# Expert weights laid out per partition, gate and up in one transfer, and the token table summed on TensorE

## The chip, the cores and the metric

The kernel runs on one core of one Trainium2 chip. The metric is the device time of one execution in microseconds (us), the median of the runs shown; lower is better.

## What is computed

A block of 512 tokens (D = 1024, float32) passes two models in a row: a mixer, a cross attention and a mixture of experts, then twice a token mixer with four branches and a mixture of experts. Only the three expert layers bear on the change. Each has 32 experts in four groups; a token goes to the best group and to the best two experts in it. An expert's hidden width is 512 in the first layer and 256 in the other two.

```python
    order = jnp.argsort(e_flat)
    e_sorted, t_sorted, w_sorted = e_flat[order], t_flat[order], w_flat[order]
...
    def expert_block(args):
        xb, e = args
        return (jax.nn.silu(xb @ w_gate[e]) * (xb @ w_up[e])) @ w_down[e]
...
    contrib = (w_sorted[:, None] * y_disp[dest].astype(jnp.float32))
    out = jnp.zeros((T, D), jnp.float32).at[t_sorted].add(contrib)
```

## The kernel before

`moe` (L770) is called three times, as e0 (L2080, hidden width FF = 512) and as e1 and e2 (L2091, FF = 256). Tokens are computed in blocks of up to 64 of one expert, so an expert with up to 64 tokens is one block. Every expert has at least one block, so all weights are read: 6 MB per expert in e0 (gate 2 MB, up 2 MB, down 2 MB), 3 MB in e1 and e2 (1 MB each).

**The router and the token table.** TensorE makes the router's logits (L963), VectorE (DVE) picks group and experts, TensorE ranks the tokens per expert (L973 to L977), and DVE turns counts into the number of blocks of each expert and their running end (`table`, L1115, L1116) and, for each of a token's two choices, into its slot: block times 64 plus place (`slotf`, L1124; `sloti`, L1125). The table of which token lies in which slot is made through DRAM: GpSimd (POOL) scatters token numbers to `token_dram` in 8 indirect DMAs (L1175), SP reads it back as `tokrow` (L918), TensorE transposes it (L981), and DVE writes the columns `tokcol` and `choicecol` (L1127 to L1131). Column n of `tokcol` names the tokens of block n.

**A block.** POOL copies a column and gathers the tokens' rows from DRAM (`gather`, L1181 to L1184) into `gathered`, a single buffer, one block ahead. TensorE transposes them (`turn`, L986, L988), DVE copies them to `xT`, TensorE multiplies with gate and up (L1008, L1010), ScalarE applies silu (L1058), DVE multiplies (L1149), TensorE transposes and multiplies with down (L1020, L1030), ScalarE copies y out (L1065), and POOL scatters it to `y_dram` (L1206). After the last block SP reads `y_dram` back (L955) and DVE adds it up.

**The weights.** They lie in a ring of RING slots: 3 in e0, 6 in e1 and e2, the last one borrowed from the tiles `h` and `hT`. In DRAM a weight is [rows, width]; partition p gets rows p, 128 + p and so on, so that a transfer consists of rows of 2 KB (gate and up in e0), 1 KB (in e1 and e2) and 4 KB (down). SP issues all of them. It first issues EARLY loads (5 in e0, 10 in e1 and e2), then stands at `token_scattered` until the eight scatters have landed, issues the `tokrow` reads, and fills the rest of the ring, each load behind the landing of the one before last (DEPTH = 2). Then `refill` runs for each expert whose slot comes free: gate for the expert RING ahead once TensorE's gate and up matmuls of this one are done, down once its down matmuls are done. Each load also waits for another to land:

```python
                    sp.wait_ge(gu_ready, end * 2)
                    sp.wait_ge(w_sem[prev][1], landed)
                    load(e + RING, s, 0)
                    sp.wait_ge(w_sem[prev][2], landed)
                    load(e + RING, s, 1)
                    sp.wait_ge(y_ready, end)
                    sp.wait_ge(w_sem[s][0], (turn_ + 2) * 16)
                    load(e + RING, s, 2)
```

`w_sem[slot]` has one semaphore for gate, up and down each, and `prev` is the slot before. TensorE's `expert` waits for all three of its slot before its first block.

## Time and profile before

| | us |
|---|---|
| median of 3 runs | 3297.98 |
| the runs | 3296.54 to 3298.09 |
| the profiled execution | 3299.51 |
| its span, first to last instruction | 3297.7 |
| TensorE (PE) busy | 2522.0, 76% |
| TensorE weight load (PEld) busy | 1944.4, 59% |
| VectorE (DVE) busy | 1129.3, 34% |
| ScalarE (ACT) busy | 942.6, 29% |
| GpSimd (POOL) busy | 382.1, 12% |
| queue of SP's DMAs | 538.84 MB, 49.0% of 16 engines |

How to read it: times are those of one profiled execution. An engine is busy while it runs an instruction; waits and DMA issues don't count. DMA share is the mean busy share of the core's 16 DMA engines; it can pass 1 by a few per cent. The granted clock (PEclk) is TensorE's, as a share of full speed; its mean is 0.875. A name like `e_wd` is a tile `wd` of any of the three layers; `m_h` and `m_hT` are the borrowed slot of e0.

### The profile page before, as it was taken

How to read it: one execution, taken by the hardware profiler on the slowest of the kernel's cores; microseconds unless marked ns; L12 is line 12 of the kernel's file. 1: busy time of each engine (PE TensorE's matmuls, PEld its weight loads, DVE VectorE, ACT ScalarE, POOL GpSimd, SP SyncE). 2: the span in 40 equal slices, each digit the busy share in tenths (PEclk: the TensorE clock that was granted, in tenths of full speed). 3: DMA queues.
4: the chain of work that ended last, by engine and by line, in shares of the span. 5: the costliest groups of instructions: out<-in, count | busy, mean ns of one | idle time of the engine just before them, and what ended most of it. 6: DMA issues, size and time to landing. Idle time of an engine off the chain costs nothing. (4 is left out here: it accounts for less than half of the span.)

```text
span 3297.7 us, 51074 instructions
## 1 busy us (share of the span) xinstructions
PE 2522.0 (76%) x17895; PEld 1944.4 (59%) x17896; DVE 1129.3 (34%) x2435; ACT 942.6 (29%) x1720; POOL 382.1 (12%) x716
## 2 busy tenths in 40 slices
PE   5974798388788758699898378884969998648882
PEld 4963698254444437576677266663847676626662
DVE  4447334210000025546543311115634753411113
ACT  2333223111112122245432123332234532213331
POOL 0000000111111110000000233331000000123332
PEclk9987899689889989799999588896979999768886
DMA  3201221599999953122121579993222121199994
GB/s 117 78 1 52 75 92 52 176 375 382 378 377 369 376 199 123 33 57 64 48 64 51 178 257 308 312 310 125 64 56 57 49 64 55 51 306 324 313 327 172
DMA packets 416210, 565.87 MB, mean 172 GB/s; under 512 B 28706, under 2 KB 303778, under 8 KB 416076
## 3 DMA queue, kind: packets, MB, share of 16 engines
q1 hardware_dynamic: 397932, 538.84, 49.0%
q0 software_dynamic: 18144, 25.24, 2.5%
q8 instruction: 85, 1.39, 0.2%
q14 instruction: 49, 0.40, 0.0%
HBM read 559.47 MB, written 35.97 MB: 181 GB/s over the span
## 5 line engine op out<-in xcount | busy, mean ns | idle before, releaser
L1008 PE MATMUL ps<-e_wg,e_xT 128*64 128x128 f32 (+1 forms) x2688 | 429.2, 322 | 78.5 <-issue 65.1
L1008 PEld LDWEIGHTS ps<-e_wg,e_xT 128*64 128x64 f32 x2688 | 344.7, 147 | 206.5 <-issue 158.3
L1010 PE MATMUL ps<-e_wu,e_xT 128*64 128x128 f32 (+1 forms) x2688 | 429.0, 322 | 0.0
L1149 DVE TENSOR_TENSOR e_hid<-e_silu,ps 64x128 f32<-64x128 f32 (+1 forms) x210 | 69.1, 334 | 947.6 <-ACT e_silu L1058 886.5
L1010 PEld LDWEIGHTS ps<-e_wu,e_xT 128*64 128x64 f32 x2688 | 344.3, 147 | 0.0
L1030 PE MATMUL ps<-e_wd,e_hidT 128*64 128x512 f32 x1112 | 304.1, 682 | 9.4 <-ACT e_hidT L1061 6.5
L1885 PE MATMUL ps<-t_hT,t1a_t1g_w 128*128 128x512 f32 x768 | 199.2, 411 | 4.6 <-DVE t1a_t1g_w L1907 2.4
L1885 PE MATMUL ps<-t_hT,t0a_t0g_w 128*128 128x512 f32 x768 | 199.2, 411 | 4.6 <-DVE t0a_t0g_w L1907 2.4
L447 POOL TENSOR_TENSOR all_x<-all_x,ln_rows 128x1024 f32<-128x1024 f32 x16 | 48.2, 3041 | 1261.4 <-DVE all_x L440 1261.4
L1058 ACT ACTIVATE e_silu<-ps 64x128 f32<-64x128 f32 (+1 forms) x210 | 62.3, 303 | 436.4 <-PE ps L1010 435.6
L1885 PEld LDWEIGHTS ps<-t_hT,t1a_t1g_w 128*128 128x128 f32 x768 | 145.4, 194 | 45.7 <-issue 10.3
L1885 PEld LDWEIGHTS ps<-t_hT,t0a_t0g_w 128*128 128x128 f32 x768 | 145.4, 194 | 45.7 <-issue 10.3
L1030 PEld LDWEIGHTS ps<-e_wd,e_hidT 128*64 128x64 f32 x1112 | 83.9, 150 | 130.1 <-issue 117.0
L1058 ACT ACT_TABLE_LOAD x105 | 134.7, 1283 | 75.6 <-issue 69.2
L1065 ACT COPY e_y<-ps 128x512 f32<-128x512 f32 x105 | 61.6, 586 | 326.8 <-PE ps L1030 240.5
L986 PE MATMUL ps<-all_ident,e_gathered 64*128 64x64 f32 x216 | 48.4, 305 | 102.7 <-DMA e_gathered<-e_dram_rows,e_tokcur 102.7
L1184 POOL DMA_INDIRECT e_gathered<-e_dram_rows,e_tokcur x111 | 112.3, 1011 | 58.6 <-issue 58.6
L1206 POOL DMA_INDIRECT e_dram_y<-e_y,e_choicecur x105 | 110.0, 1048 | 57.0 <-issue 57.0
L986 PEld LDWEIGHTS ps<-all_ident,e_gathered 64*128 64x128 f32 x216 | 33.2, 192 | 131.5 <-DMA e_gathered<-e_dram_rows,e_tokcur 83.7
L1175 POOL DMA_INDIRECT e_dram_token<-all_choice,e_sloti x24 | 23.5, 977 | 710.0 <-DVE e_sloti L1125 703.6
L1008 PE MATMUL ps<-m_h,e_xT 128*64 128x256 f32 x320 | 82.9, 424 | 28.2 <-issue 28.2
L1020 PE MATMUL ps<-all_ident,e_hid 64*128 64x64 f32 x556 | 92.5, 293 | 0.5 <-DVE e_hid L1149 0.3
(595 smaller groups left out, 4696.0 us busy)
## 6 DMA issues: line engine op xcount, KB each, us to landing
e_wd<-in_w_down SPq DMA_DIRECT2D x32, 2048.0 KB
e_wd<-in_w_exp_down SPq DMA_DIRECT2D x64, 1024.0 KB
e_wg<-in_w_exp_gate SPq DMA_DIRECT2D x54, 1024.0 KB
e_wu<-in_w_exp_up SPq DMA_DIRECT2D x54, 1024.0 KB
e_wg<-in_w_gate SPq DMA_DIRECT2D x22, 2048.0 KB
e_wu<-in_w_up SPq DMA_DIRECT2D x22, 2048.0 KB
m_h<-in_w_gate SPq DMA_DIRECT2D x10, 2048.0 KB
m_hT<-in_w_up SPq DMA_DIRECT2D x10, 2048.0 KB
```

The source lines that it names most:

```text
L447: nc.gpsimd.tensor_tensor(x[:, t, :], x[:, t, :], rows[:, 1], ALU.add).then_inc(shifted, 1)
L986: nc.tensor.matmul(ps_turn[:, 0:SLOTS], gathered[:, 0:P], ident[0:SLOTS, 0:SLOTS], start=True, stop=True)
L1008: nc.tensor.matmul(ps_gu[q][0:SLOTS], xT[:, c, :], wg[s][:, c, span], start=c == 0, stop=c == DC - 1)
L1010: last = nc.tensor.matmul(ps_gu[q][SLOTS:P], xT[:, c, :], wu[s][:, c, span], start=c == 0, stop=c == DC - 1)
L1020: last = nc.tensor.matmul(ps_hid[q][:, f * SLOTS:(f + 1) * SLOTS], hid[SLOTS:P, q, f * P:(f + 1) * P], ident[SLOTS:P, SLOTS:P], start=True ...
L1030: last = nc.tensor.matmul(ps_y[h * SLOTS:(h + 1) * SLOTS], hidT[:, f, :], wd[s][:, f, h * 512:(h + 1) * 512], start=f == 0, stop=f == NF - 1)
L1058: nc.scalar.activation(silu[SLOTS:P, q], ps_gu[q][0:SLOTS], ACT.Silu).then_inc(silu_ready, 1)
L1065: nc.scalar.copy(y[:], ps_y).then_inc(y_copied, 1)
L1149: vec.tensor_tensor(hid[SLOTS:P, q], silu[SLOTS:P, q], ps_gu[q][SLOTS:P], ALU.mult).then_inc(hid_ready, 1)
L1184: nc.gpsimd.indirect_dma_start(gathered[:], None, rows_dram, bass.IndirectOffsetOnAxis(tokcur[:], 0), bounds_check=S - 1, oob_is_err=False ...
L1206: nc.gpsimd.indirect_dma_start(y_dram, bass.IndirectOffsetOnAxis(choicecur[:], 0), y[:], None, bounds_check=4 * S - 1, oob_is_err=False).t ...
L1885: last = nc.tensor.matmul(ps[:, 6, :], w[:, p, q, :], self.hT[:, r, q, :], start=q == 0 and p == r, stop=q == DC - 1 and p == LO)
```

## The change

- The weights' arrays are laid out anew before the launch (`by_partition`), so that all that one partition gets of an expert is one contiguous run: gate and up together, 32 KB in e0 and 16 KB in e1 and e2, and down, 16 KB and 8 KB. The bytes are the same.
- Gate and up are one transfer into one tile `wgu`, with one semaphore. An expert has two loads instead of three. EARLY is 3 in e0 and 6 in e1 and e2, 10 MB as before in e0 and 9 MB instead of 10 in e1 and e2. In `refill`, the wait and load in the middle are gone and the other lines stand as they were; `w_sem[prev][1]` is now the semaphore of the previous slot's down.
- The token table is no longer made through DRAM. DVE splits a slot into block and place, writes rows of 0 and 1 (`at_pos`: place is s; `at_blk`: block is b, times the token's number plus 1), and TensorE sums their products over the tokens in 16 matmuls, 64 x 50 each, into `ps_tok` (eight per half of the partitions). The eight scatters, the `tokrow` reads, SP's wait for the scatters and the fill of `token_dram` are gone.

```diff
-                         ("iota_e", [P, NE], F32), ("group_of", [P, NE], F32), ("choice", [P, 2, TT], F32), ("second", [P, 1], F32)):
+                         ("iota_e", [P, NE], F32), ("group_of", [P, NE], F32), ("iota_pos", [P, SLOTS], F32), ("iota_blk", [P, TABLE], F32), ("choice", [P, 2, TT], F32), ("second", [P, 1], F32)):
...
+            g.memset(k["second"][:], -2.0)
...
-            g.iota(k["choice"][:], [[S, 2], [P, TT]], 0, 1, allow_small_or_imprecise_dtypes=True).then_inc(made, 1)
+            g.iota(k["iota_pos"][:], [[1, SLOTS]], 0, 0, allow_small_or_imprecise_dtypes=True)
+            g.iota(k["iota_blk"][:], [[1, TABLE]], 0, 0, allow_small_or_imprecise_dtypes=True)
+            g.iota(k["choice"][:], [[S, 2], [P, TT]], 1, 1, allow_small_or_imprecise_dtypes=True).then_inc(made, 1)
...
-def moe(nc, name, k, x, hT, h_rows, gain, w_rg, b_rg, w_re, b_re, w_gate, w_up, w_down, alpha=1.0):
+def moe(nc, name, k, x, hT, h_rows, gain, w_rg, b_rg, w_re, b_re, w_gate_up, w_down, spare, alpha=1.0):
...
-    EARLY = 5 * 512 // FF
+    EARLY = 3 * 512 // FF
...
-        wg_own = st.sb("wg", [P, OWN, DC, FF])
-        wu_own = st.sb("wu", [P, OWN, DC, FF])
+        wgu_own = st.sb("wgu", [P, OWN, 2, DC, FF])
         wd_all = st.sb("wd", [P, RING, NF, D])
-        if FF == 512:
-            borrowed = [h_rows.rearrange("p t (c f) -> p (t c) f", f=FF), hT[:]]
-        else:
-            half = DC // 2
-            borrowed = [hT[:, n * half:(n + 1) * half].rearrange("p c (q f) -> p (c q) f", f=FF) for n in range(2)]
-        wg = [wg_own[:, s] for s in range(OWN)] + borrowed[0:1]
-        wu = [wu_own[:, s] for s in range(OWN)] + borrowed[1:2]
+        wgu = [wgu_own[:, s] for s in range(OWN)] + [spare.rearrange("p (m c f) -> p m c f", m=2, f=FF)]
         wd = [wd_all[:, s] for s in range(RING)]
...
                 def load(e, s, m):
-                    w, dram = ((wg, wg_dram), (wu, wu_dram), (wd, wd_dram))[m]
-                    sp.dma_start(w[s], dram[bass.ds(e, 1)].rearrange("e p c f -> p (e c) f")).then_inc(w_sem[s][m], 16)
+                    if m == 0:
+                        sp.dma_start(wgu[s].rearrange("p m c f -> p (m c f)"),
+                                     w_gate_up[bass.ds(e, 1)].rearrange("e p m c f -> p (e m c f)")).then_inc(w_sem[s][0], 16)
+                    else:
+                        sp.dma_start(wd[s].rearrange("p c f -> p (c f)"),
+                                     w_down[bass.ds(e, 1)].rearrange("e p c f -> p (e c f)")).then_inc(w_sem[s][1], 16)
 
...
-                sp.wait_ge(zero_ready, 1)
-                sp.dma_start(token_dram.rearrange("(b s) one -> b (s one)", s=SLOTS), zero[:]).then_inc(zero_stored, 16)
                 sp.dma_start(rows_dram.rearrange("(t p) d -> p t d", p=P), h_rows).then_inc(rows_stored, 16)
-                first = [(s, m) for s in range(RING) for m in range(3)]
-                first = [(s, m) for s in range(RING) for m in range(3)]
+                first = [(s, m) for s in range(RING) for m in range(2)]
                 for s, m in first[:EARLY]:
                     load(s, s, m)
 
-                sp.wait_ge(token_scattered, 16 * 2 * TT)
-                for q in range(2):
-                    sp.dma_start(tokrow[:, q], token_dram.rearrange("(b s) one -> b (s one)", s=SLOTS)).then_inc(tokrow_landed, 16)
                 for n in range(EARLY, len(first)):
                     done_s, done_m = first[n - DEPTH]
                     sp.wait_ge(w_sem[done_s][done_m], 16)
-                    if n == 3 * OWN:
+                    if n == 2 * OWN:
 
                         sp.wait_ge(logitsT_ready, 1)
                         sp.wait_ge(rows_stored, 16)
...
                     sp.wait_ge(gu_ready, end * 2)
                     sp.wait_ge(w_sem[prev][1], landed)
                     load(e + RING, s, 0)
-                    sp.wait_ge(w_sem[prev][2], landed)
-                    load(e + RING, s, 1)
                     sp.wait_ge(y_ready, end)
                     sp.wait_ge(w_sem[s][0], (turn_ + 2) * 16)
-                    load(e + RING, s, 2)
+                    load(e + RING, s, 1)
...
-                pe.wait_ge(tokrow_landed, 32)
-                nb = TABLE
-                nc.tensor.transpose(ps_tok, tokrow[:].rearrange("b q s -> b (q s)"), ident[0:nb, 0:nb]).then_inc(tokT_ready, 1)
+                pe.wait_ge(hot_slots_ready, 1)
+                for j in range(2):
+                    for t in range(TT):
+                        for q in range(2):
+                            last = nc.tensor.matmul(ps_tok[q * SLOTS:(q + 1) * SLOTS], at_pos[:, j, t, :], at_blk[:, j, t, :],
+                                                    start=j + t == 0, stop=j + t == TT)
+                last.then_inc(tokT_ready, 1)
...
-                    for m in range(3):
+                    for m in range(2):
...
-                vec.tensor_copy(sloti[:], slotf[:]).then_inc(table_ready, 1)
+                link(vec.tensor_scalar(blk_up[:], slotf[:], 1.0 / SLOTS, 0.5 / SLOTS - 0.5, ALU.mult, ALU.add))
+                link(vec.tensor_scalar(blk_up[:], blk_up[:], ROUND, None, ALU.add))
+                link(vec.tensor_scalar(blk[:], blk_up[:], -ROUND, None, ALU.add))
+                link(vec.scalar_tensor_tensor(pos[:], blk[:], -float(SLOTS), slotf[:], ALU.mult, ALU.add))
+                vec.tensor_tensor(at_pos[:].rearrange("p j t s -> p (j t) s"),
+                                  k["iota_pos"][:].unsqueeze(1).to_broadcast([P, 2 * TT, SLOTS]),
+                                  pos[:].rearrange("p j t -> p (j t)").unsqueeze(2).to_broadcast([P, 2 * TT, SLOTS]),
+                                  ALU.is_equal)
+                flat = at_blk[:].rearrange("p j t b -> p (j t) b")
+                link(vec.tensor_tensor(flat, k["iota_blk"][:].unsqueeze(1).to_broadcast([P, 2 * TT, TABLE]),
+                                       blk[:].rearrange("p j t -> p (j t)").unsqueeze(2).to_broadcast([P, 2 * TT, TABLE]),
+                                       ALU.is_equal))
+                vec.tensor_tensor(flat, flat, k["choice"][:].rearrange("p j t -> p (j t)").unsqueeze(2).to_broadcast(
+                    [P, 2 * TT, TABLE]), ALU.mult).then_inc(hot_slots_ready, 1)
                 dve.wait_ge(tokT_ready, 1)
-                link(vec.tensor_scalar(part[:, 0], ps_tok, 1.0, None, ALU.mult))
-                link(vec.tensor_scalar(part[:, 1], part[:, 0], float(S), float(-S), ALU.is_ge, ALU.mult))
-                link(vec.tensor_tensor(part[:, 2], part[:, 0], part[:, 1], ALU.add))
-                vec.tensor_scalar(choicecol[:], part[:, 0], 2.0, k["second"][:], ALU.mult, ALU.add).then_inc(tokcol_ready, 1)
-                vec.tensor_copy(tokcol[:], part[0:SLOTS, 2]).then_inc(tokcol_ready, 1)
+                vec.tensor_scalar(part[:, 0], ps_tok, 1.0, float(4 * S + 2), ALU.is_lt, ALU.mult)
+                vec.tensor_scalar(part[:, 1], ps_tok, float(S), float(-S), ALU.is_gt, ALU.mult)
+                link(vec.tensor_scalar(part[:, 2], ps_tok, 2.0, k["second"][:], ALU.mult, ALU.add))
+                link(vec.scalar_tensor_tensor(part[:, 3], ps_tok, -1.0, part[:, 1], ALU.add, ALU.add))
+                vec.tensor_tensor(choicecol[:], part[:, 2], part[:, 0], ALU.add).then_inc(tokcol_ready, 1)
+                vec.tensor_tensor(tokcol[:], part[0:SLOTS, 3], part[0:SLOTS, 0], ALU.add).then_inc(tokcol_ready, 1)
...
-                pool.wait_ge(zero_stored, 16)
                 pool.wait_ge(rows_stored, 16)
-                pool.wait_ge(table_ready, 3)
-                for t in range(TT):
-                    for j in range(2):
-                        nc.gpsimd.indirect_dma_start(token_dram, bass.IndirectOffsetOnAxis(sloti[:, j, t:t + 1], 0),
-                                                     k["choice"][:, j, t:t + 1], None).then_inc(token_scattered, 16)
+                pool.wait_ge(table_ready, 2)
                 pool.wait_ge(tokcol_ready, 2)
...
+def by_partition(w):
+
+    layers, experts, rows, width = w.shape
+    return w.reshape(layers, experts, rows // P, P, width).transpose(0, 1, 3, 2, 4)
...
+    for n in ("", "_2"):
+        stem = "w_exp_" if n else "w_"
+        arrays[f"{stem}gate_up{n}"] = np.ascontiguousarray(np.stack(
+            [by_partition(inputs[f"{stem}{m}{n}"]) for m in ("gate", "up")], axis=3))
+        arrays[f"{stem}down{n}"] = np.ascontiguousarray(by_partition(inputs[f"{stem}down{n}"]))
```

The first place is SP's queue in the loop of `refill`s of e0, slots 1 and 2, before. The lines with `[waits ...]` name semaphores by the first name that their number had in the program: here rope_dve_chain, rope_ready and rope_sined are the landings of slot 0's up, slot 0's down and slot 1's gate, and mixn_act_chain, mixn_landed and mixw_bank_full those of slot 1's up, slot 1's down and slot 2's gate.

```order
L903 ISA [waits rope_dve_chain,e0_gate_up_ready]
L903 DMA e_wg<-in_w_gate 128x8x512
L903 DMA e_wu<-in_w_up 128x8x512 [waits rope_ready]
L903 DMA e_wd<-in_w_down 128x4x1024 [waits rope_sined,e0_y_ready]
L932 ISA
L932 TENSOR_LOAD e_table
L932 ISA x2
L935 REGISTER_ALU
L903 ISA [waits mixn_act_chain,e0_gate_up_ready]
L903 DMA m_h<-in_w_gate 128x8x512
L903 DMA m_hT<-in_w_up 128x8x512 [waits mixn_landed]
L903 DMA e_wd<-in_w_down 128x4x1024 [waits mixw_bank_full,e0_y_ready]
```

The same place now. Here rope_dve_chain, rope_ready, rope_sined and mixn_act_chain are the landings of slot 0's down, slot 1's gate and up, slot 1's down, and slot 2's gate and up.

```order
L894 ISA [waits rope_dve_chain,e0_gate_up_ready]
L894 DMA e_wgu<-in_w_gate_up 128x8192
L897 ISA [waits rope_ready,e0_y_ready]
L897 DMA e_wd<-in_w_down 128x4096
L922 ISA
L922 TENSOR_LOAD e_table
L922 ISA x2
L925 REGISTER_ALU
L894 ISA [waits rope_sined,e0_gate_up_ready]
L894 DMA m_both<-in_w_gate_up 128x8192
L897 ISA [waits mixn_act_chain,e0_y_ready]
L897 DMA e_wd<-in_w_down 128x4096
```

Three loads of an expert have become two. Before, each load waited for the one before last; now each waits for the load just ahead of it.

The second place is POOL's queue in e0 from the layer's start to the gather of the first block, before:

```order
L1175 DMA e_dram_token<-all_choice,e_sloti 3200x1 [waits e0_table_ready,mixw_turn_high_ready,mixh_dve_chain]
L1175 DMA e_dram_token<-all_choice,e_sloti 3200x1 x7
L1188 DMA e_dram_spare<-all_ident 16x1x4 [waits e0_tokcol_ready]
L1181 COPY e_tokcur<-e_tokcol 64x1 [waits e0_gathered_cleared]
L1168 TENSOR_TENSOR e_aside<-all_ident 1x1 [waits e0_tokcur_ready]
L1184 DMA e_gathered<-e_dram_rows,e_tokcur 64x1024
L1181 COPY e_tokcur<-e_tokcol 64x1 [waits e0_turned]
```

And now:

```order
L1188 DMA e_dram_spare<-all_ident 16x1x4 [waits e0_tokcol_ready,e0_table_ready,mixw_emptied_by_act]
L1181 COPY e_tokcur<-e_tokcol 64x1 [waits e0_gathered_cleared]
L1173 TENSOR_TENSOR e_aside<-all_ident 1x1 [waits e0_tokcur_ready]
L1184 DMA e_gathered<-e_dram_rows,e_tokcur 64x1024
L1181 COPY e_tokcur<-e_tokcol 64x1 [waits e0_turned]
```

The eight scatters ahead of the first gather are gone; POOL goes on as soon as the token columns are ready.

## Rows read from the trace of the kernel before

**Rows 1.** the page's 40 slices of the span (82.4 us each): DMA share in tenths, GB/s

```profile
DMA  3201221599999953122121579993222121199994
GB/s 117 78 1 52 75 92 52 176 375 382 378 377 369 376 199 123 33 57 64 48 64 51 178 257 308 312 310 125 64 56 57 49 64 55 51 306 324 313 327 172
```

**Rows 2.** windows of 50 us in e0, e1, e2; the first line names the columns

```profile
core 0: us, PE busy (x) PEld busy (x) DVE busy (x) ACT busy (x) POOL busy (x), PEclk, DMA share, GB/s
750.00:800.00 50.00, 39.75 (x291) 22.81 (x291) 4.62 (x9) 10.75 (x20) 9.71 (x21) 0.93 1.04 380
2050.00:2100.00 50.00, 43.91 (x505) 32.44 (x505) 7.59 (x19) 16.88 (x36) 16.54 (x36) 0.90 0.99 320
3050.00:3100.00 50.00, 42.95 (x497) 31.52 (x493) 6.38 (x16) 16.32 (x34) 16.07 (x34) 0.89 1.02 323
```

**Rows 3.** waits in e0, 668 to 1180 us: total us, times, longest us

```profile
PE ps L1008 <- issue: 90.5, 24, 7.6
...
SPq L903 <- DMA e_wd<-in_w_down: 141.4, 29, 6.1
```

**Rows 4.** waits in e1, 1860 to 2300 us

```profile
PE ps L986 <- DMA e_gathered<-e_dram_rows,e_tokcur: 47.9, 25, 9.8
...
SPq L903 <- PE ps L1010: 22.7, 3, 14.2
```

**Rows 5.** timeline of SP's queue, e0: start us, us, instruction

```profile
677.43 0.40 SPq L903 DMA_DIRECT2D e_wg<-in_w_gate  x1
...
1169.25 0.37 SPq L903 DMA_DIRECT2D e_wu<-in_w_up  x1
```

**Rows 6.** timeline of ScalarE, e0: copies of y, the first two and the last

```profile
682.44 0.59 ACT L1065 COPY e_y<-ps 128x512 f32<-128x512 f32 x1 [3.41 <-PE ps L1030]
...
694.51 0.59 ACT L1065 COPY e_y<-ps 128x512 f32<-128x512 f32 x1 [3.40 <-PE ps L1030]
...
1208.51 0.59 ACT L1065 COPY e_y<-ps 128x512 f32<-128x512 f32 x1 [3.40 <-PE ps L1030]
```

**Rows 7.** timeline in e1 and e2: a refill's gate load, the last y copy

```profile
1962.04 0.38 SPq L903 DMA_DIRECT2D e_wg<-in_w_exp_gate  x1
...
2235.67 0.59 ACT L1065 COPY e_y<-ps 128x512 f32<-128x512 f32 x1 [1.91 <-PE ps L1030]
...
2953.90 0.40 SPq L903 DMA_DIRECT2D e_wg<-in_w_exp_gate  x1
...
3245.99 0.59 ACT L1065 COPY e_y<-ps 128x512 f32<-128x512 f32 x1 [1.92 <-PE ps L1030]
```

**Rows 8.** windows around the memory load issued at 375.01; the read of y

```profile
375.01:376.04 1.03, 0.00 (x0) 0.00 (x0) 0.00 (x0) 1.00 (x2) 0.00 (x0) 1.00 0.00 0
376.05:379.55 3.50, 0.00 (x0) 0.00 (x0) 0.00 (x0) 3.41 (x8) 0.00 (x0) 0.78 0.91 298
1213.90:1225.34 11.44, 0.00 (x0) 0.00 (x0) 8.36 (x7) 0.00 (x0) 0.00 (x0) 0.50 0.95 367
```

**Rows 9.** DMA issues by tile: count, KB each, us from issue to landing

```profile
e_router<-in_w_router_group SPq DMA_DIRECT2D x2, 16.0 KB, 2.4
```

**Rows 10.** timeline of the token table in e0

```profile
638.75 0.17 DVE L1125 CAST e_sloti<-e_slotf 128x8 uint32<-128x8 f32 x1
...
648.88 0.96 POOL L1175 DMA_INDIRECT e_dram_token<-all_choice,e_sloti  x1 [0.30 <-issue]
...
656.93 0.18 DVE L1131 CAST e_tokcol<-e_part 64x50 uint32<-64x50 f32 x1
...
666.31 0.66 PE L986 MATMUL ps<-all_ident,e_gathered 64*128 64x64 f32 x2 [10.29 <-DMA e_gathered<-e_dram_rows,e_tokcur]
```

**Rows 11.** timeline in e0: nearest rows for the added DVE and TensorE work

```profile
632.69 1.89 PE L977 MATMUL ps<-e_both,all_ones 128*128 128x32 f32 x8
...
636.92 0.18 DVE L1118 TENSOR_SCALAR e_ends<-e_ends 128x32 f32<-128x32 f32 x1
...
667.76 0.69 DVE L1139 TENSOR_TENSOR e_xT<-ps,all_columns 128x512 f32<-128x512 f32 x1 [10.65 <-PE ps L988]
```

More of the change, by code:

```diff
@@ L28 @@
 TABLE = MAX_BLOCKS + 2
-ROWS = TABLE * SLOTS
+ROUND = 12582912.0
 class Stage:
@@ L748, in _ @@
                 g.memset(k[n][:], 1.0)
-            for n in ("ident", "mask_le", "mask_lt", "mask_ge", "second"):
+            for n in ("ident", "mask_le", "mask_lt", "mask_ge"):
                 g.memset(k[n][:], 0.0)
+            g.memset(k["second"][:], -2.0)
             g.iota(k["iota_e"][:], [[1, NE]], 0, 0, allow_small_or_imprecise_dtypes=True)
@@ L753, in _ @@
                    allow_small_or_imprecise_dtypes=True)
[L754 removed]
+            g.iota(k["iota_pos"][:], [[1, SLOTS]], 0, 0, allow_small_or_imprecise_dtypes=True)
+            g.iota(k["iota_blk"][:], [[1, TABLE]], 0, 0, allow_small_or_imprecise_dtypes=True)
+            g.iota(k["choice"][:], [[S, 2], [P, TT]], 1, 1, allow_small_or_imprecise_dtypes=True).then_inc(made, 1)
             pool.wait_ge(made, 1)
[L756 removed]
+            g.affine_select(k["second"][:], k["second"][:], [[0, 1]], ALU.is_ge, -1.0, SLOTS - 1, -1)
             g.affine_select(k["ident"][:], k["ident"][:], [[-1, P]], ALU.not_equal, 1.0, 0, 1)
@@ L827, in moe @@
         slotf = st.sb("slotf", [P, 2, TT])
-        sloti = st.sb("sloti", [P, 2, TT], U32)
+        blk = st.sb("blk", [P, 2, TT])
+        blk_up = st.sb("blk_up", [P, 2, TT])
+        pos = st.sb("pos", [P, 2, TT])
+        at_pos = st.sb("at_pos", [P, 2, TT, SLOTS])
+        at_blk = st.sb("at_blk", [P, 2, TT, TABLE])
         table = st.sb("table", [1, 2, NE], I32)
-        zero = st.sb("zero", [TABLE, SLOTS])
-        tokrow = st.sb("tokrow", [TABLE, 2, SLOTS])
-        part = st.sb("part", [P, 3, TABLE])
+        part = st.sb("part", [P, 4, TABLE])
         tokcol = st.sb("tokcol", [SLOTS, TABLE], U32)
@@ L844, in moe @@
         aside = st.sb("aside", [1, 1])
-        w_sem = [[st.sem(f"{m}_landed{s}") for m in ("gate", "up", "down")] for s in range(RING)]
+        w_sem = [[st.sem(f"{m}_landed{s}") for m in ("gate_up", "down")] for s in range(RING)]
         router_landed = st.sem("router_landed")
         rows_stored = st.sem("rows_stored")
-        zero_ready = st.sem("zero_ready")
-        zero_stored = st.sem("zero_stored")
         logits_ready = st.sem("logits_ready")
@@ L879, in moe @@
         back_used = st.sem("back_used")
-        wg_dram = w_gate.rearrange("e (c p) f -> e p c f", p=P)
-        wu_dram = w_up.rearrange("e (c p) f -> e p c f", p=P)
-        wd_dram = w_down.rearrange("e (c p) d -> e p c d", p=P)
         ps_turn = ps[:, 0, :]
@@ L1007, in expert @@
                             for c in range(DC):
-                                nc.tensor.matmul(ps_gu[q][0:SLOTS], xT[:, c, :], wg[s][:, c, span],
+                                nc.tensor.matmul(ps_gu[q][0:SLOTS], xT[:, c, :], wgu[s][:, 0, c, span],
                                                  start=c == 0, stop=c == DC - 1)
-                                last = nc.tensor.matmul(ps_gu[q][SLOTS:P], xT[:, c, :], wu[s][:, c, span],
+                                last = nc.tensor.matmul(ps_gu[q][SLOTS:P], xT[:, c, :], wgu[s][:, 1, c, span],
                                                         start=c == 0, stop=c == DC - 1)
@@ L1071, in _ @@
                 vec = nc.vector
-                vec.memset(zero[:], float(2 * S)).then_inc(zero_ready, 1)
                 vec.memset(gathered[:], 0.0).then_inc(gathered_cleared, 1)
@@ L2074, in program @@
             with Stage(nc, "m3") as s3:
-                h = s3.sb("h", [P, TT, D])
-                hT = s3.sb("hT", [P, DC, S])
+                both = s3.sb("both", [P, 2, TT * D])
+                h = both[:, 0].rearrange("p (t d) -> p t d", t=TT)
+                hT = both[:, 1].rearrange("p (c s) -> p c s", c=DC)
                 rms_rows(nc, "m3n", [(lambda t: x[:, t, :], lambda t: h[:, t, :], TT, D)], 1e-6)
@@ L2079, in program @@
                      [plain(nc, hT[:, c, :], col("g_moe")[:, c:c + 1]) for c in range(DC)])
-                moe(nc, "e0", k, x, hT, h[:], col("g_moe"), i["w_rg"][0], i["b_rg"][0], i["w_re"][0], i["b_re"][0],
-                    i["w_gate"][0], i["w_up"][0], i["w_down"][0])
+                moe(nc, "e0", k, x, hT, h, col("g_moe"), i["w_rg"][0], i["b_rg"][0], i["w_re"][0], i["b_re"][0],
+                    i["w_gate_up"][0], i["w_down"][0], both[:].rearrange("p m n -> p (m n)"))
             final_norm(nc, "m4", x, gain_row("g_final"), 1e-6)
```

21 lines of the change are left out of this document (9 added, 12 removed).

## The prediction

> **What bounds the kernel now.** I looked first at the slices of the span [rows 1]. The DMA engines are full in three stretches, near 0.6 to 1.17 ms, 1.9 to 2.2 ms and 2.9 to 3.25 ms, and nowhere else. These are the three expert layers e0, e1 and e2, and only they are touched by the change. Then I cut windows out of them [rows 2]: the DMA share is 0.99 to 1.04 in each, but the bytes per second differ, 380 GB/s in e0 and 320 and 323 GB/s in e1 and e2. The reader is to see that the same full engines move fewer bytes where a gate or up row is 1 KB (e1, e2) than where it is 2 KB (e0); rows of w_down are 4 KB in all three.
>
> Next the waits. In e0 TensorE waits 90.5 us at the first gate matmul of 24 blocks, which is a wait for weights, and SP waits 141.4 us for w_down alone [rows 3]: transfers follow one another and the rest waits for them. In e1 TensorE waits besides for gathered tokens, 47.9 us in 25 blocks, and SP was once held 14.2 us by TensorE, because the first experts of e1 have two and three blocks [rows 4]. So e0 and e2 are bound by weight transfers, e1 by them from its ninth expert on.
>
> **What a refill costs now.** Each `refill` issues three loads and every load waits for the one before last, so one transfer is always under way while the next is issued. In e0 expert 3's gate is issued at 677.43 and expert 31's up, released by expert 30's down, at 1169.25 [rows 5]: 28 experts in 491.8 us, about 17.5 us each. The last y copy is at 1208.51, 39.3 us after that release: expert 30 has two blocks and a block takes 12.1 us (682.44 to 694.51) [rows 6]. In e1 expert 8's gate is issued at 1962.04 and the last y copy is at 2235.67; in e2 expert 6's gate goes at 2953.90 and the last copy is at 3245.99 [rows 7].
>
> **The change, part by part.** (1) *Handover.* This is the part on which I stake the sign. The order was g0 u0 d0 g1 with waits two back. Joining gate and up removed the middle load and its wait, but gate_up still waits for `w_sem[prev][1]`, which now is the down of the slot before, the transfer issued immediately before it; and down waits for the gate_up immediately before it. Every refill transfer now starts after the previous one has landed. The order of SP's queue shows it: three waits and three loads per expert became two loads, each behind the semaphore of the load just ahead. What a start from nothing costs, the trace shows away from the experts [rows 8]: the memory load issued at 375.01 moves nothing in its first 1.03 us, and its 1 MB ends at 379.55, 4.54 us in all; at 400 GB/s 1.05 MB would be 2.62 us, so 1.9 us are fixed even without the landing and SP's next step. A 16 KB load takes 2.4 us from issue to landing, nearly all of it fixed [rows 9]. I take g = 2.5 us per transfer: the 2.4 and a tenth for SP to go on; the ends are 1.9 and 3.0.
>
> (2) *Longer rows.* A partition's run becomes 32 KB and 16 KB in e0, 16 KB and 8 KB in e1 and e2. No row of this trace has such a run, so I bound the rate. With a cost per byte of 1/R + c/row, e0 (mean of 1/row 0.417 per KB, 380 GB/s [rows 2]) and e1/e2 (0.75, 321.5 GB/s) give c = 0.0014 and R near 490; for rows cut at 4 KB that makes 418 GB/s, for the uncut ones some 470. Against it stands the read of y, all in 4 KB rows: 4 MB at 367 GB/s [rows 8]. I take 400, between e0's mixed 380 and the extrapolated 418. One expert of e1 or e2 is 3.146 MB, x = 7.86 us; of e0 twice that. With two handovers an expert costs a = 2x + 2g = 20.7 us in e0 and b = x + 2g = 12.9 us in e1 and e2, beside 17.5 and at most 11.2 now (e2: 292.1 us over 26 experts, the last block in it). The gathers and y stores (about 0.5 MB per block at most) I let fall into the gaps, at nothing; if they do not, they add some 0.5 us to an expert, inside the upper end.
>
> A rule bears on both parts. The rows give 1.9 to 2.4 us fixed, and 298 to 380 GB/s. The Trainium skill ("DMA: Bandwidth & Descriptors", section "Anatomy of one DMA") gives a fit for one DMA from GpSimd's queue of about 2.0 us plus bytes at 436 GB/s; as an estimate from that page the whole sum below would be +9 us, 3307 us, the second rival. The trace's solo 1 MB load took 4.54 us where that fit says 4.4, so they nearly agree for that one.
>
> (3) *The token table.* Eight scatters on GpSimd (1.26 us apart), a read back and a transposition go; DVE and TensorE work comes instead. Before, from the cast of the slots at 638.75 to the finished token columns at 657.11 are 18.4 us, and the first turn comes at 666.31 [rows 10]. Now: four small DVE operations at 0.18 us and their gap, 0.8 us; three wide ones (512, 400 and 400 elements) bounded by the 0.69 us of a 512-element one, 1.9 us; 16 matmuls with 64 weight columns, between 0.24 and 0.47 us each (eight records, of four matmuls with 128 columns, took 1.89 us; half the columns may take half), taken as 0.3, 4.8 us; six short DVE steps, some back to back, 1.1 us [rows 11]. That is 8.6 us, so the first turn is 9.8 us earlier, 10 in all three layers. The gather behind it keeps its price. SP no longer stands behind the scatters, so the first ring (18.9 MB) is loaded without a gap, but that only covers: it has landed by about 665 in e0 (issued from 612 on, 47 us at 400 GB/s, and some 6 for the 2 MB of token rows written beside it), just before the first refill may go (667.7, because the first gate and up matmuls end 10 us earlier). The two added iotas and the removed 50-row memset are under 1 us at the start, hidden beside the first loads: nothing.
>
> **The sum.** e0: first refill at 667.7, 28 experts to the landing of expert 30's down, then 39.3 us: 667.7 + 28a + 39.3 - 1208.5 = 28a - 501.5; with a = 20.7, +78. e1: TensorE still holds expert 8 back, so it goes at 1952; 24 experts, then some 10 us for the last block, a little under the 11.2 an expert takes now: 1952 + 24b + 10 - 2235.7 = 24b - 273.7, +36. e2: 2944 + 26b + 10 - 3246 = 26b - 292, +43. Together +157 us; in one line the sum is 106x + 156g - 1067. TensorE's blocks (12.1 us in e0; in e1 and e2 an expert, with all its waits, takes 11.2 now) stay shorter than an expert's transfers, and so does the gather's round, so the transfers alone set the end. The profiled execution took 3299.5 us, 1.5 more than the median; on the median of 3298.0 the forecast is **3455 us**. Its own range: x 7.53 (418 GB/s) with g 2.1 gives +59, x 8.28 (380) with g 3.0 gives +278: 3357 to 3576.
>
> **Rivals.** *Faster (0.09):* long runs are so quick that the lost overlap is paid for. With the extrapolated 470 GB/s (x = 6.69) and g = 1.9, the sum is -62, 3236 us. It decides in the refills, from x = 7.3 (433 GB/s) down at g = 1.9, or from 6.4 at 2.5. For it speaks the step from 321.5 to 380 GB/s; against it, that no slice of this trace moves more than 382 [rows 1], and that the solo load had only 298 GB/s while it ran. *About even (0.07, of which 0.03 within 0.2%):* g = 1.9 to 2.0, just what the solo load shows, and x = 7.2 (437 GB/s, between 418 and 470): -8 to +8, 3290 to 3306 us. *Far slower (0.14):* long runs bring nothing, or the gathers' 4 KB rows queue behind 16 and 32 KB ones: at e0's present 359 GB/s of weights (6.29 MB in 17.5 us), x = 8.76, +251, 3549 us. A late gather adds to this only where a block would take longer than 12.9 us, 2 us more than now. *It doesn't do what it says:* if SP still ran two transfers deep, a would be 15.7, and b 7.86 and half of the 1.9 us that a late gather costs in e1 now, 8.8: -62, -62 and -63, 3111 us. The two wait lines speak plainly against it; its chance is within the 0.09.
>
> **How the numbers follow.** The forecast has 0.70. Slower by over 0.2% (about what a measurement of this kernel can tell from no change): 0.70 + 0.14 + 0.04 = 0.88; within it 0.03; faster 0.09. The range takes in the forecast's ends and reaches a little towards the even case: 3345 to 3575.
>
> **What would show it.** Right: the DMA share of a window in e0 falls from 1.04 to about 0.76 and in e1 and e2 to about 0.61, with a dead stretch before each load; SP waits for gate_up and down in turn, issues of gate_up are 20.7 and 12.9 us apart; the first turn is 10 us nearer to the layer's start; TensorE waits some 8 us per expert in e0. Wrong: a share near 1 (two loads under way after all), 470 GB/s while a load runs, or gate_up issues under 18 us apart in e0.

## The result, and the profile after

| kernel | median us | runs | ratio to before, 95% interval |
|---|---|---|---|
| before | 3297.3 | 4, 3295.5 to 3298.1 | |
| changed | 3522.1 | 4, 3518.4 to 3523.5 | 1.0681 (1.0662 to 1.0699) |

The change makes the kernel 225 us slower. The forecast was 3455, +157; its sign and its range (3345 to 3575) held, its size was 68 us short.

The page's 40 slices of the changed kernel (88 us each), DMA share in tenths and GB/s, and its line on SP's queue:

```profile
DMA  3201212878888864122121767764112122477764
GB/s 110 73 1 49 96 61 62 338 303 313 306 305 306 305 228 138 54 53 61 45 60 60 275 217 250 253 243 143 61 53 60 51 55 78 154 286 253 264 246 160
...
q1 hardware_dynamic: 191056, 538.71, 43.0%
```

The 9s of [rows 1] are gone: the engines are 7 to 8 tenths busy in e0 and 6 to 7 in e1 and e2, over longer stretches, and carry the same bytes (538.71 MB, 538.84 before). Windows of 50 us, the first at the place of e0's in [rows 2], the others in e1 and e2:

```profile
core 0: us, PE busy (x) PEld busy (x) DVE busy (x) ACT busy (x) POOL busy (x), PEclk, DMA share, GB/s
750.00:800.00 50.00, 34.11 (x239) 18.73 (x235) 4.20 (x8) 8.57 (x17) 7.22 (x17) 0.86 0.78 298
2100.00:2150.00 50.00, 44.15 (x526) 33.33 (x528) 8.35 (x20) 17.32 (x38) 17.79 (x39) 0.97 0.71 258
3150.00:3200.00 50.00, 40.33 (x433) 30.96 (x434) 6.92 (x16) 14.45 (x32) 14.27 (x33) 0.86 0.72 257
```

GB/s over DMA share is 382 in e0, where [rows 2] give 365, and 363 and 357 where they give about 320: long rows do move more while the DMA engines run. The granted clock fell too, to 0.86 from 0.93 in the window of e0, but TensorE stands waiting for weights there, as the waits below show. What is lost is between the loads, as the timeline of SP's queue in e0 shows (start us, us, instruction):

```profile
803.91 0.34 SPq L894 DMA_DIRECT2D e_wgu<-in_w_gate_up  x1
816.37 0.33 SPq L897 DMA_DIRECT2D e_wd<-in_w_down  x1
824.39 0.34 SPq L894 DMA_DIRECT2D e_wgu<-in_w_gate_up  x1
...
844.98 0.34 SPq L894 DMA_DIRECT2D m_both<-in_w_gate_up  x1
```

Here a gate_up takes 12.5 us until its down is issued and a down 8.0 until the next gate_up; over e0 (790 to 1160 us) the medians are 12.6 and 8.7, so 2.1 and 3.5 us more than their bytes at 400 GB/s. These intervals are about the time a load takes to land. The list of DMA issues has it for the 4 MB gate_up of e0 and for the gate_up of e1 and e2, which at 2 MB is as large as e0's down (tile, count, KB each, us to landing):

```profile
e_wgu<-in_w_exp_gate_up SPq DMA_DIRECT2D x54, 2048.0 KB, 8.0
e_wgu<-in_w_gate_up SPq DMA_DIRECT2D x22, 4096.0 KB, 12.4
```

Windows around the down issued at 816.37 and the gate_up issued at 824.39:

```profile
814.90:816.37 1.47, 1.47 (x9) 0.57 (x10) 0.03 (x1) 0.27 (x1) 0.95 (x2) 1.00 0.01 0
816.37:817.00 0.63, 0.63 (x4) 0.14 (x2) 0.00 (x0) 0.00 (x0) 0.12 (x1) 1.00 0.00 0
817.00:817.40 0.40, 0.40 (x4) 0.14 (x2) 0.00 (x0) 0.00 (x0) 0.00 (x0) 1.00 1.00 143
817.40:823.60 6.20, 1.10 (x6) 0.14 (x2) 0.00 (x0) 1.87 (x2) 1.40 (x3) 0.81 0.93 358
823.90:824.39 0.49, 0.00 (x0) 0.00 (x0) 0.00 (x0) 0.00 (x0) 0.00 (x0) 0.50 0.03 8
824.39:825.30 0.91, 0.02 (x2) 0.03 (x2) 0.00 (x0) 0.00 (x0) 0.00 (x0) 0.50 0.00 0
```

Nothing moves in the last 1.47 us before the down's issue, nor in the 0.63 us after it: 2.1 us. From 817.00 on bytes move again; a gather had been issued at 815.49, and the trace doesn't say whether the first of them are the gather's or the down's. Then come 358 GB/s. At the gate_up, behind the shorter down, the dead stretch is only 1.4 us. The two are no exceptions: in windows of 0.1 us around the 20 issues of each kind from 780 to 1200 us, the stretch with a DMA share under a tenth has a median of 2.6 us at a down (1.7 before the issue, 0.9 behind it) and of 1.3 us at a gate_up (0.4 and 0.9). So 3.9 us of an e0 expert are dead, not twice the forecast's g of 2.5. The waits of TensorE and SP in e0, 668 to 1300 us (total, times, longest):

```profile
PE ps L1000 <- issue: 174.2, 26, 9.4
...
SPq L926 <- DMA e_wd<-in_w_down: 149.4, 20, 8.3
SPq L929 <- DMA e_wgu<-in_w_gate_up: 134.1, 11, 13.8
SPq L929 <- DMA m_both<-in_w_gate_up: 109.4, 9, 12.9
```

SP waits for gate_up and down in turn, where it waited above all for w_down [rows 3], and TensorE's wait for weights grew from 90.5 us in 24 blocks to 174.2 in 26, from 3.8 to 6.7 us each. The token table in e0:

```profile
640.72 0.17 DVE L1116 TENSOR_SCALAR e_blk_up<-e_slotf 128x8 f32<-128x8 f32 x1
...
643.38 1.95 PE L971 MATMUL ps<-e_at_blk,e_at_pos 128*64 128x50 f32 x32 [6.83 <-DVE e_at_blk L1128]
...
646.29 0.20 DVE L1136 TENSOR_TENSOR e_tokcol<-e_part 64x50 uint32<-64x50 f32 x1
...
649.00 1.05 POOL L1184 DMA_INDIRECT e_gathered<-e_dram_rows,e_tokcur  x1 [0.65 <-issue]
...
660.60 0.66 PE L978 MATMUL ps<-all_ident,e_gathered 64*128 64x64 f32 x2 [15.26 <-DMA e_gathered<-e_dram_rows,e_tokcur]
```

The columns are ready 5.8 us after the slots (18.4 in [rows 10]), but from the gather's issue to the first turn are now 11.6 us, where it was 7.3 (659.04 to 666.31). In e1 it is 7.6 us (6.8 before) and in e2 5.3 (7.1 before), so the delay is large in e0 alone.

**Where the time went.** For every kernel below: us per expert is the time from the issue of expert 12's first load to that of expert 28's, over 16; the last y copy is counted from the layer's first router load. All are read from the profiled executions' timelines. A ratio is to the kernel before as timed beside that kernel: 3297.3 us for the changed one, 3294.7 for after_two_deep and the three kernels that start from the one before, 3300.7 for one_handover and the two with rows cut at 4 KB, 3302.6 for other_handover and long_rows_and_table.

| kernel | ratio | us per expert e0 / e1 / e2 | last y copy e0 / e1 / e2 |
|---|---|---|---|
| before | | 17.47 / 10.82 / 10.94 | 599.5 / 390.4 / 362.7 |
| changed | 1.068 | 21.43 / 13.59 / 13.45 | 702.8 / 446.6 / 423.4 |
| after_two_deep | 0.985 | 16.32 / 9.63 / 9.97 | 562.5 / 379.7 / 351.6 |
| one_handover | 1.042 | 19.05 / 12.37 / 12.32 | 642.8 / 444.1 / 413.2 |
| other_handover | 1.021 | 18.26 / 11.65 / 11.90 | 615.7 / 416.9 / 384.4 |
| before_one_deep | 1.159 | 25.74 / 16.48 / 16.58 | 833.2 / 520.0 / 516.7 |
| before_long_rows | 0.985 | 16.27 / 9.36 / 9.49 | 570.0 / 380.0 / 340.8 |
| before_table_only | 0.992 | 17.42 / 10.53 / 10.90 | 589.2 / 377.2 / 360.8 |
| after_4k | 1.088 | 22.38 / 14.49 / 14.59 | 725.8 / 466.3 / 459.8 |
| two_deep_4k | 0.981 | 16.82 / 9.70 / 9.43 | 571.3 / 380.8 / 340.2 |
| long_rows_and_table | 0.973 | 16.31 / 9.45 / 9.83 | 558.1 / 369.9 / 334.9 |

The three layers are longer by 103, 56 and 61 us: 220 of the 225.

### The profile page after: what moved, and what is told of

Read it like the earlier page. It is cut to its first block and busy times, and to the rows that moved or that the text cites. A ratio compares the mean times of both kernels' runs of the same rounds, so it can differ in the third digit from the quotient of the medians.

```text
span 3519.9 us, 51151 instructions
## 1 busy us (share of the span) xinstructions
PE 2579.8 (73%) x17988; PEld 1999.2 (57%) x17989; DVE 1136.3 (32%) x2453; ACT 943.6 (27%) x1720; POOL 357.4 (10%) x694
## 3 DMA queue, kind: packets, MB, share of 16 engines
q1 hardware_dynamic: 191056, 538.71, 43.0%
## 5 line engine op out<-in xcount | busy, mean ns | idle before, releaser
L1000 PE MATMUL ps<-e_wgu,e_xT 128*64 128x128 f32 (+1 forms) x2688 | 488.3, 351 | 257.0 <-issue 238.8
L1000 PEld LDWEIGHTS ps<-e_wgu,e_xT 128*64 128x64 f32 x2688 | 390.7, 164 | 395.3 <-issue 351.3
L1002 PE MATMUL ps<-e_wgu,e_xT 128*64 128x128 f32 (+1 forms) x2688 | 488.2, 351 | 0.0
L1002 PEld LDWEIGHTS ps<-e_wgu,e_xT 128*64 128x64 f32 x2688 | 390.6, 164 | 0.0
L1022 PE MATMUL ps<-e_wd,e_hidT 128*64 128x512 f32 x1112 | 279.1, 633 | 8.2 <-ACT e_hidT L1053 3.1
L1000 PE MATMUL ps<-m_both,e_xT 128*64 128x256 f32 x320 | 88.4, 445 | 59.4 <-issue 59.4
L1000 PEld LDWEIGHTS ps<-m_both,e_xT 128*64 128x64 f32 x320 | 51.0, 162 | 98.8 <-issue 82.4
L1181 POOL COPY e_tokcur<-e_tokcol 64x1 uint32 (+1 forms) x111 | 19.9, 179 | 813.6 <-PE ps L980 812.2
## 6 DMA issues: line engine op xcount, KB each, us to landing
e_wgu<-in_w_gate_up SPq DMA_DIRECT2D x22, 4096.0 KB, 12.4
```

Source lines behind the costliest of these rows:

```text
L1000: nc.tensor.matmul(ps_gu[q][0:SLOTS], xT[:, c, :], wgu[s][:, 0, c, span], start=c == 0, stop=c == DC - 1)
L1002: last = nc.tensor.matmul(ps_gu[q][SLOTS:P], xT[:, c, :], wgu[s][:, 1, c, span], start=c == 0, stop=c == DC - 1)
L1022: last = nc.tensor.matmul(ps_y[h * SLOTS:(h + 1) * SLOTS], hidT[:, f, :], wd[s][:, f, h * 512:(h + 1) * 512], start=f == 0, stop=f == NF - 1)
```

## The experiments

**The two waits put back.** The whole change, but every refill load waits for the one before last.

```diff
-                    sp.wait_ge(w_sem[prev][1], landed)
+                    sp.wait_ge(w_sem[prev][0], landed)
                     load(e + RING, s, 0)
                     sp.wait_ge(y_ready, end)
-                    sp.wait_ge(w_sem[s][0], (turn_ + 2) * 16)
+                    sp.wait_ge(w_sem[prev][1], landed)
                     load(e + RING, s, 1)
```

> The changed kernel with the two waits of a refill moved one load back, so that two loads are under way again. Handover theory: an expert in e0 falls from 21.3 us to about 16, in e1 and e2 from 13.5 to 9 or 9.5 (the gather's round then bounds), so the whole is 3110 to 3200 us, faster than before the change. Rival, long rows are slow themselves (their packets took 5 to 15 per cent longer than at best) or hold up the gathers: it stays above 3400 us.

Measured 3243.1, ratio 0.985 (0.983 to 0.987). SP's queue in e0, and two windows:

```profile
912.97 0.34 SPq L894 DMA_DIRECT2D e_wgu<-in_w_gate_up  x1
918.04 0.33 SPq L897 DMA_DIRECT2D e_wd<-in_w_down  x1
928.92 0.34 SPq L894 DMA_DIRECT2D e_wgu<-in_w_gate_up  x1
```

```profile
750.00:800.00 50.00, 47.35 (x366) 27.62 (x364) 6.16 (x12) 12.03 (x23) 10.81 (x24) 0.97 1.01 408
2100.00:2150.00 50.00, 42.30 (x478) 30.70 (x476) 7.36 (x17) 15.44 (x34) 15.01 (x33) 0.90 0.84 326
```

Two moved waits are worth 279 us, more than the whole loss; the rest of the change is a gain. The total lies above the expected 3200, though the times per expert came close (16.3, 9.6 and 10.0 us), because in e1 and e2 the transfers now end early: in the second window the DMA share is 0.84, and from the issue of the last gate_up to the last y copy are 45.7 us in e1 (23.7 from that of the last gate before). From one y copy to the next are 8.6 and 9.0 us on average over e1 and e2, hardly less than the 8.6 and 9.1 before. I read this as the round of a block setting the end there; what in the round does it is not shown. TensorE waited 37.6 us for gathered tokens before 17 blocks between 1900 and 2200 us, but with quarter gathers (below) the average is still 8.5 and 8.4 us.

**The kernel before, one load deep.** The opposite test: old rows, old table, three loads, each waiting for the one just ahead.

```diff
-                    sp.wait_ge(w_sem[prev][1], landed)
-                    load(e + RING, s, 0)
                     sp.wait_ge(w_sem[prev][2], landed)
+                    load(e + RING, s, 0)
+                    sp.wait_ge(w_sem[s][0], (turn_ + 2) * 16)
                     load(e + RING, s, 1)
                     sp.wait_ge(y_ready, end)
-                    sp.wait_ge(w_sem[s][0], (turn_ + 2) * 16)
+                    sp.wait_ge(w_sem[s][1], (turn_ + 2) * 16)
                     load(e + RING, s, 2)
```

> The kernel before, old layout and three loads, with each refill load waiting for the load just ahead of it: only the overlap is taken away. Handover theory: three handovers of 2.5 to 3 us per expert come in where one transfer used to cover them, e0 from 17.5 to about 24 us per expert, e1 and e2 from 11 to about 17, the whole 3700 to 3850 us. Rival, the order of waits is not what costs: under 3350 us.

Measured 3815.5, ratio 1.159 (1.157 to 1.161). The handover is the cost, with or without the other parts. A 2 MB load takes 25.74/3 = 8.58 us here and a 1 MB one 16.53/3 = 5.51 (e1 and e2). If both move at one rate, the second MB costs 3.07 us and 2.4 us are fixed, close to the 2.5 of the forecast. They need not: by the rates of [rows 2], 380 and about 320 GB/s, the fixed part would be 3.1 us in e0 and 2.2 in e1 and e2. Either way it holds what the gathers and y stores beside the loads cost.

**The rows alone, the table alone.** The kernel before with only one run per partition in DRAM (three loads, two under way), and with only the summed token table.

```diff
-    sp.dma_start(w[s], dram[bass.ds(e, 1)].rearrange("e p c f -> p (e c) f"))
+    sp.dma_start(w[s].rearrange("p c f -> p (c f)"),
+                 dram[bass.ds(e, 1)].rearrange("e p c f -> p (e c f)"))
```

> The kernel before with only the layout changed: gate, up and down each one run per partition (16 KB in e0 and 8 KB in e1 and e2), three loads, two under way. Handover theory: the long rows gain by themselves, 5 to 10 per cent per expert in e0, more in e1 and e2: 3180 to 3250 us. Rival, long rows are slow or hold up gathers: 3298 us or more.

> The kernel before with only the token table made by matmuls. It should bring the first turn 10 us forward in each expert layer; e0 and e2 are bound by transfers, which here also lose their gap behind the scatters: 3265 to 3285 us. If the table's DVE and TensorE work cost as much as the scatters did: 3298 us within 3.

Measured 3243.5, ratio 0.985 (0.984 to 0.987), and 3270.0, 0.992 (0.990 to 0.994). Both are gains, as expected: 51 and 25 us beside 3294.7. The rows' windows in e0 and e1:

```profile
750.00:800.00 50.00, 43.37 (x315) 24.84 (x317) 4.62 (x9) 9.46 (x18) 8.01 (x18) 0.90 1.00 399
2100.00:2150.00 50.00, 43.48 (x553) 33.76 (x549) 8.14 (x20) 18.34 (x39) 17.52 (x37) 0.97 0.94 350
```

399 GB/s at a share of 1.00 is the 400 that the forecast took.

**One handover at a time.** First only gate_up's wait put back, then only down's. Each leaves one start from an empty queue per expert.

```diff
# one_handover
-                    sp.wait_ge(w_sem[prev][1], landed)
+                    sp.wait_ge(w_sem[prev][0], landed)
                     load(e + RING, s, 0)
# other_handover
-                    sp.wait_ge(w_sem[s][0], (turn_ + 2) * 16)
+                    sp.wait_ge(w_sem[prev][1], landed)
                     load(e + RING, s, 1)
```

> The changed kernel with only the wait ahead of gate_up moved one load back; down still waits for the gate_up just ahead, so one handover per expert is left instead of two. If each handover costs the same, it gives back half of the 279 us between the changed kernel and its two-deep form: 3375 to 3390 us, an expert in e0 near 18.8 us. Rival, an engine is already full once one handover is covered: 3243 to 3300 us.

> The changed kernel with only the down load's wait moved: it waits for the down before it and so goes right behind gate_up, while gate_up still waits for the down just ahead. One handover per expert is left, the one at gate_up. With the other handover covered the kernel took 3442, with both 3243, with none 3522. Theory 1 (a dry queue costs the same wherever it falls, and what is left of it after one is covered is most of the cost): 3425 to 3455 again, e0 near 19 us per expert. Theory 2 (the dear one is down's wait for the long gate_up): the queue is refilled just there, so 3310 to 3350, e0 near 17 us per expert.

Measured 3442.5, ratio 1.042 (1.039 to 1.045), and 3371.1, ratio 1.021 (1.018 to 1.024). Of the 279 us that both give back, gate_up's gives 80 and down's 151. Either time lies outside both ranges expected for it: the two handovers are not alike, and neither is the whole loss. SP's queue in one_handover and in other_handover:

```profile
933.45 0.33 SPq L897 DMA_DIRECT2D e_wd<-in_w_down  x1
934.76 0.34 SPq L894 DMA_DIRECT2D m_both<-in_w_gate_up  x1
952.66 0.33 SPq L897 DMA_DIRECT2D e_wd<-in_w_down  x1
```

```profile
931.32 0.34 SPq L894 DMA_DIRECT2D m_both<-in_w_gate_up  x1
931.89 0.33 SPq L897 DMA_DIRECT2D e_wd<-in_w_down  x1
949.55 0.34 SPq L894 DMA_DIRECT2D e_wgu<-in_w_gate_up  x1
```

So an e0 expert with one handover costs 3.3 or 2.5 us beyond the 15.7 of its bytes at 400 GB/s, with two 5.7. The handover after a gate_up costs some 0.8 us more than the one after a down. The traces show where this lies: between 780 and 1200 us the stretch with a DMA share under a tenth has a median of 2.7 us at a down's issue in one_handover, and is there at all 22. At a gate_up's issue in other_handover it is 1.4 us, and at 6 of the 23 other transfers fill it. The difference is in the time before the issue (1.8 against 0.6 us), not in the time from the issue to the next bytes (0.9 in both). Why the last bytes of the long gate_up come so long before SP goes on stays open.

**The rows cut at 4 KB.** The joined loads as they are, but each 4 KB in DRAM followed by 256 bytes of padding, so that no row is longer, and the loads read only the 4 KB; once with two loads under way and once with one.

```diff
+def apart(w):
+    w = w.reshape(*w.shape[:3], -1, D)
+    return np.ascontiguousarray(np.pad(w, [(0, 0)] * 4 + [(0, 64)]))
...
```

> The two-deep form with every DRAM run broken into 4 KB rows by a gap of 256 bytes; transfers, waits and bytes are the same. Theory that 8 to 32 KB rows hold up the rows of GpSimd's gathers and y stores: the first turn in e0 comes within 6 us of its gather's issue instead of 10.5, and the whole is 3210 to 3235 us. Rival, only the transfers' rate counts and 4 KB rows cost 3 to 4 per cent of it: 3250 to 3265 us.

> The changed kernel with its one-deep waits and 4 KB rows. Handover theory: the waits cost nearly what they did, 3490 to 3540 us. Rival, part of the slowdown is the long rows holding up other DMAs: under 3470 us.

Measured 3236.5, ratio 0.981 (0.978 to 0.984), and 3592.8, ratio 1.088 (1.085 to 1.091). With two under way e0's rate falls a little:

```profile
750.00:800.00 50.00, 40.59 (x295) 23.01 (x291) 4.62 (x9) 10.08 (x20) 8.41 (x19) 0.93 1.02 394
```

and the first turn comes earlier; the two about cancel, and the total, a little below the 3243.1 of after_two_deep, is just above the first expectation; the first turn came 7.0 us after its gather's issue, not within 6. The gather's issue and the first turn of e0 in two_deep_4k:

```profile
645.01 1.05 POOL L1183 DMA_INDIRECT e_gathered<-e_dram_rows,e_tokcur  x1 [0.65 <-issue]
...
652.01 0.66 PE L977 MATMUL ps<-all_ident,e_gathered 64*128 64x64 f32 x2 [10.66 <-DMA e_gathered<-e_dram_rows,e_tokcur]
```

Issue to turn of e0's first gather is 7.0 us here and in after_4k. In the other kernels with full gathers it goes by the rows of the loads that fill the ring just then: 6.8 to 8.1 us with rows of 2 and 4 KB (before, before_table_only, before_one_deep), 9.1 and 8.8 with 16 KB (before_long_rows, long_rows_and_table), 11.0 to 12.5 with 32 KB gate_up rows (changed, after_two_deep, one_handover, other_handover). The load's size is the same in two_deep_4k and after_two_deep, so it is the length of the rows already queued that the gather waits behind. In e1 and e2, whose gate_up rows are 16 KB, the same time spreads from 5.3 to 11.9 us, against 4.9 to 8.0 with rows of up to 4 KB.

The second kernel missed its expectation: one load deep, short rows cost 0.9 to 1.1 us more per expert, e1 and e2 as much as e0, though their loads are half as long. It behaves like a dearer handover, and the trace shows a part: in e0 1.3 us pass between a gate_up's issue and the next bytes, where it was 0.9. The rest is open.

**Smaller gathers.** Each gather fetches 1 KB of 4 KB per token, once with two loads under way and once in the changed kernel itself; its blocks then work on other data than they should.

```diff
-nc.gpsimd.indirect_dma_start(gathered[:], None, rows_dram, ...
+nc.gpsimd.indirect_dma_start(gathered[:, 0:D // 4], None,
+                             rows_dram.rearrange("s (q d) -> (s q) d", q=4), ...
```

> The two-deep form with each gather fetching 1 KB per token instead of 4 KB, into the first quarter of the buffer, so that blocks work on other data than they should. If in e1 and e2 the gather's round bounds a block now (8.6 and 9.0 us from one y copy to the next), it falls to 8 us or less and the whole is 3215 us or less. If weights or TensorE bound them: 3235 us or more.

> The changed kernel, but each gather fetches 1 KB of a token's 4 KB, so the blocks work on other data and part of the gather is left out; the blocks of e1 and e2 change with it, so e0's time per expert is what is compared (21.43 us in the changed kernel; with two loads under way the same cut took it from 16.32 to 15.26). Theory 1 (the gathers' bytes fall into the gaps between the weight loads, at nothing, as the prediction had it, and the handover itself is 2.8 us): 21.2 to 21.5. Theory 2 (the gathers share the queue's busy stretches, and the excess over the forecast's 20.7 is theirs): 20.3 to 20.7.

One execution each: 3187.3 and 3470.3, beside 3300.7 and 3293.7 of the kernel before. The totals include other block counts; e0 compares. Per expert it takes 15.26 us (16.32 with full gathers) and 20.58 (21.43). Windows of after_small_gather in e0:

```profile
750.00:800.00 50.00, 32.44 (x226) 18.52 (x228) 3.08 (x6) 6.30 (x12) 5.97 (x13) 0.80 0.80 311
1000.00:1050.00 50.00, 36.51 (x266) 20.95 (x264) 3.56 (x8) 7.05 (x14) 5.46 (x12) 0.83 0.81 324
```

Nearly the same share (0.78 and 0.80 in the changed kernel's same two windows) moves more weights. The gathers do not fall into the gaps: three quarters of them cost 0.85 us per expert even where the queue runs dry twice, and 1.06 where it doesn't. Their bytes alone (0.2 MB per block at 400 GB/s) would be 0.5. In e1 and e2 the first kernel went against its expectation: a block's round did not fall to 8 us or less.

**All but the joined load.** The rows and the table, but three loads and the old waits.

> The kernel before with the rows per partition and the summed token table, but with three loads per expert and its old waits (two under way): everything of the change but the joined load and its waits. Long rows alone took 3243.5, the table alone 3270.0 (28 less than before), the two and the joined load with two under way 3243.1. Theory 1 (the parts add, and the joined 4 MB load cost what the table had gained): 3212 to 3225. Theory 2 (long rows hold back the first gather, so the table gains little beside them, joined or not): 3232 to 3245, with 10 us from the gather's issue to the first turn.

Measured 3211.0, ratio 0.973 (0.971 to 0.975): faster than both kernels and than every other one here that does the whole work. The parts add and a little more: 92 us beside 3302.6, where the rows gave 51 and the table 25. The joined load, which costs 279 us by its waits, costs another 32 when these are mended (3243.1). The first y copies are 4.8, 8.1 and 5.0 us earlier here, and the last ones 4.4, 9.8 and 16.7. That the 32 KB rows hold the first gather 3 us longer explains most of e0's part; the rest is not explained.

```profile
647.66 1.04 POOL L1189 DMA_INDIRECT e_gathered<-e_dram_rows,e_tokcur  x1 [0.65 <-issue]
...
656.50 0.66 PE L983 MATMUL ps<-all_ident,e_gathered 64*128 64x64 f32 x2 [12.49 <-DMA e_gathered<-e_dram_rows,e_tokcur]
```

## Why the prediction was right in kind and short in size

**The mechanism was right.** That the joined load's wait is for the transfer just ahead, and that each transfer then starts from an empty queue, is what the issues of SP show, what after_two_deep takes away and before_one_deep brings back. *It doesn't do what it says* (3111) fell by SP's waits for the load just ahead, and *faster* (3236) because no 50 us window read from any run moves more than 422 GB/s, where it needed 470. *About even* needed 437 GB/s and fixed costs of at most 2.0. *Far slower* (3549) lies nearest in microseconds but not in cause: it had a rate of 359, and x was not at fault. Its other ground, gathers that queue behind long rows, is real in e0 (11.6 us for 7.3), but without the long rows the kernel is slower still (3592.8).

**The rate was right.** a - b is 21.43 - 13.52 = 7.91 us for 3.146 MB, 398 GB/s; the forecast had 400 and x = 7.86.

**The mis-sized term is g.** By a = 2x + 2g with x = 7.91, g is 2.8 instead of 2.5. The forecast's sum, 106x + 156g - 1067, then gives +208 instead of +157; by the measured a and b directly, 98 + 53 + 58 = +209. What failed is the sentence that gathers and y stores "fall into the gaps, at nothing": with gathers cut to a quarter a is 20.58, and the forecast was 20.7. The sentence after it, that they would add some 0.5 us "if they do not", had the right cause and too small a price; its own 0.5 MB per block would be 1.3 us at 400 GB/s.

That 20.58 meets 20.7 so well is partly luck. The y stores, as large as full gathers, were still whole in that run, and the dead stretches of the changed kernel are 2.6 and 1.3 us, 3.9 per expert, where the forecast had 5.0. So g = 2.5 was too much for the dead time alone, and the traffic beside it took up the rest: of the 5.7 us that an e0 expert takes beyond its bytes, 3.9 are dead and some 1.8 are not.

**The remaining 16 us** are 4.8, 3.7 and 3.0 in the three layers (measured 103.3, 56.2 and 60.7 against 98.5, 52.5 and 57.7) and 5 outside them. In e0 and e1 they are mostly the first refill, which the sum held fixed: expert 3's load is issued 62.6 us after the layer's start and not 58.7, expert 8's 110.6 and not 106.7. In e2 expert 6's goes at 60.7, just as forecast; there an expert takes 13.58 us over all refills, not 13.45. The first turn was to come 10 us earlier and came 6.6 us earlier in e0. The table's own work was overpriced (16 matmuls took 1.95 us, not 4.8; 5.8 us in all, not 8.6), so 12.6 us were won there, but "the gather behind it keeps its price" failed: 11.6 us for 7.3. The first y copy is 5.7 us nearer the layer's start in e0 (67.7 for 73.4), 8.7 in e1 and 17.3 in e2, where the gather took 5.3 us. The 5 us outside the layers were not assigned.

**By the signs that were named.** DMA share in e0 0.78 (forecast 0.76), in e1 and e2 0.71 and 0.72 (0.61, too low; the likely reason is that gathers and y stores, counted as nothing, weigh more per byte of weights there). Gate_up issues 21.4 and 13.5 us apart (20.7 and 12.9). TensorE's waits 6.7 us at each stop (8).

The Trainium skill ("DMA: Bandwidth & Descriptors", section "Anatomy of one DMA") gives a fit for one DMA from GpSimd's queue, by which the sum came to 3307 us as an estimate, against 3522 measured. For the two big loads, which SP issues, its fit says 11.6 us (4096 KB) and 6.8 (2048 KB); landing took 12.4 and 8.0 to 8.1. That is 0.8 and 1.2 us low per transfer, and the traffic beside them, which the fit doesn't have, may be among the reasons.

## What to carry to other kernels

When loads are merged, read again which transfer each wait names: "one before last" in a list of three becomes "the one just ahead" in a list of two, and cost 2.4 to 2.8 us per transfer here, the traffic beside it included, on a stream that sets the end. Keep two under way, and give each change of layout its own run: here two good parts (−51 and −25 us) hid behind a third. Count small transfers on other queues at full price and more, even where the main queue has gaps. Look at the row length of bulk loads that lie ahead of the first gather of a layer; 4 KB rows brought it forward by 5 us in e0, but the whole kernel by only 7 (3236.5 for 3243.1).
